# Where the first memory-key product stands: in the head loop, or among the latent products

## What is computed

```
kv  = (rmsnorm(ckv, kv_norm) @ w_ukv)           # latent products: k_nope, v of latent attention
k_c = gelu(flat @ w1) @ w2                      # compression: first product, gelu, second product
p_c = softmax(q . k_c ...)                      # compressed branch, before the head loop
s, p = scores and softmax of 3 x 6 heads        # the head loop, 18 turns
kvm = rmsnorm(mem, g_mem) @ wkv                 # memory keys and values, needed first by cross-attention
```

## Time and profile before

| | |
|---|---|
| median of 3 runs | 1771.8 us (1768.76 to 1776.57) |
| the profiled execution's own time | 1768.37 us |
| its span | 1766.5 us |
| PE busy | 1674.3 us (95%) |
| DVE busy | 1361.8 us (77%) |
| ACT busy | 1081.1 us (61%) |
| POOL busy | 210.6 us (12%) |
| mean granted clock of TensorE | 0.976 |

### The profile page before, as it was taken

How to read it: one execution, slowest core, us unless ns; L and a number is a source line. 1 busy time by engine, 2 the same in 40 slices (tenths; PEclk the granted TensorE clock), 3 DMA queues, 4 the chain that set the end, 5 groups by cost and what they waited for, 6 DMA issues and landing times.

```text
span 1766.5 us, 24349 instructions
## 1 busy us (share of the span) xinstructions
PE 1674.3 (95%) x8492; PEld 1399.3 (79%) x8492; DVE 1361.8 (77%) x1529; ACT 1081.1 (61%) x1188; POOL 210.6 (12%) x234
## 2 busy tenths in 40 slices
PE   5899999999988999969999999999999999999995
PEld 5868888888786888858888888888888888888784
DVE  5866656545577756559898898988989999989895
ACT  4345444434353454437777777777777777777773
POOL 1834001000066410030000000000000000000200
PEclk8989999999988999989999999999999999999998
DMA  9401443955431124339999999999999999999992
GB/s 356 169 24 58 151 150 140 373 190 190 176 134 48 49 97 166 119 111 423 380 374 385 373 381 369 375 385 373 374 387 371 393 378 361 389 372 356 416 375 84
DMA packets 68697, 475.94 MB, mean 269 GB/s; under 512 B 7543, under 2 KB 9079, under 8 KB 13976
## 3 DMA queue, kind: packets, MB, share of 16 engines
q1 hardware_dynamic: 63816, 453.01, 67.3%
q0 software_dynamic: 4816, 22.08, 3.1%
HBM read 461.82 MB, written 13.24 MB: 269 GB/s over the span
## 4 chain that ended last, share of the span: by engine, by line
PE 81%; DVE 7%; ACT 4%; POOL 3%; issue 2%; DMA 2%; DVEq 0%; POOLq 0%; ACTq 0%; SPq 0%
PE bank L431 24%; PE bank L433 23%; PE bank L432 23%; POOL big L2254 1%; ACT upper L474 1%; PE bank L623 1%; DVE lower L455 1%; DMA skewed_bias<-big 1%; ACT upper L451 1%; PE bank L1395 1%; DVE xel L964 1%; PE bank L1493 1%; POOL small L2254 1%; PE bank L1285 1%; PE bank L1394 1%
## 5 line engine op out<-in xcount | busy, mean ns | idle before, releaser
L480 DVE TENSOR_TENSOR lower<-ring,upper 128x2048 fp32r<-128x2048 f32 x369 | 845.4, 2292 | 144.7 <-ACT upper L474 131.5
L474 ACT ACTIVATE upper<-ring 128x2048 fp32r<-128x2048 f32 x369 | 706.4, 1915 | 108.8 <-PE bank L433 102.6
L431 PE MATMUL bank<-upper,xeu 128*128 128x512 f32 x896 | 359.7, 401 | 6.6 <-DVE xel L964 3.4
L433 PE MATMUL bank<-upper,xel 128*128 128x512 f32 x896 | 350.5, 391 | 0.0
L432 PE MATMUL bank<-lower,xeu 128*128 128x512 f32 x896 | 349.5, 390 | 0.0
L431 PE MATMUL bank<-upper,htu 128*128 128x512 f32 x536 | 209.7, 391 | 4.9 <-DVE htl L978 3.4
L433 PE MATMUL bank<-upper,htl 128*128 128x512 f32 x536 | 208.6, 389 | 0.0
L432 PE MATMUL bank<-lower,htu 128*128 128x512 f32 x536 | 208.6, 389 | 0.0
L431 PEld LDWEIGHTS bank<-upper,xeu 128*128 128x128 f32 x896 | 168.3, 188 | 38.8 <-DVE lower L480 4.1
L433 PEld LDWEIGHTS bank<-upper,xel 128*128 128x128 f32 x896 | 168.2, 188 | 35.9
L432 PEld LDWEIGHTS bank<-lower,xeu 128*128 128x128 f32 x896 | 168.7, 188 | 31.8
(11 more groups left out here) (381 smaller groups left out, 2553.6 us busy)
## 6 DMA issues: line engine op xcount, KB each, us to landing
ring<-in_weights SPq DMA_DIRECT2D x423, 1024.0 KB, 5.9
routed_rows<-g POOLq DMA_DIRECT2D x1, 4096.0 KB, 36.7
lp<-in_lparams POOLq DMA_DIRECT2D x1, 3634.5 KB, 14.4
lp<-in_lparams SPq DMA_DIRECT2D x1, 3584.0 KB, 29.5
memraw<-routed_rows POOLq DMA_DIRECT2D x7, 512.0 KB, 8.2
expert_rows<-xk POOLq DMA_DIRECT2D x7, 512.0 KB, 8.4
skewed_bias<-big SPq DMA_DIRECT2D x1, 1152.0 KB, 19.4
row<-in_mem SPq DMA_DIRECT2D x1, 1024.0 KB, 5.1
```

Source lines behind the costliest of these rows:

```text
L431: pe.matmul(to, x_up, w_up, start=start, stop=False, skip_group_check=True)
L433: return pe.matmul(to, x_lo, w_up, start=False, stop=stop, skip_group_check=True)
L474: act.activation(upper[:, third(q), :], ring[:, q % RING, :], ACT.Copy).then_inc(done, 1)
L480: dve.tensor_tensor(lower[:, q % RING, :], ring[:, q % RING, :], f32(upper[:, third(q), :]), ALU.subtract).then_inc(done, 1)
```

## The change

The job `mk0` moves in the list from turn 2 of the head loop to the place between `vm1` and `kcv`. PE: the wait for the memory's split columns and the product of chunk 7 now stand after `vm1`, ahead of the wait for `hid_ready`. ACT: the upper part of chunk 7 after the copy of `kwT`, the copy of `mk0` after `hidr`. DVE: the lower part of chunk 7 after the second rotation, ahead of `states(1)`. The splits of chunks 8 to 11 stay in turns 2, 6, 10 and 14.

```diff
@@ JOBS
-               ("vm1", "act"), ("kcv", "dve"), ("bu2", "dve"), ...
+               ("vm1", "act"), ("mk0", "act"), ("kcv", "dve"), ("bu2", "dve"), ...
-    _job(_n, _e)
+    _job(_n, _e, 7 if _n == "mk0" else None)
...
-MEMK = {2: 0, 6: 1, 10: 2, 14: 3}
+MEMK = {6: 1, 10: 2, 14: 3}
+MEM_SPLIT = {2: 1, 6: 2, 10: 3, 14: 4}
@@ PE
                     finish(f"vm{t}", ins)
+                pe.wait_ge(mem_split[l], KD)
+                features_out("mk0", MEM_FIRST, colr, memr)
                 pe.wait_ge(hid_ready[l], 1)
...
                 for i in range(LEAD):
                     scores(i)
-                pe.wait_ge(mem_split[l], KD)
@@ ACT
+                def memory_keys(m):
+                    wait_tile(act, l, f"mk{m}")
+                    drained(A(xk[:, 2 * m:2 * m + 2, :], bank(f"mk{m}")[:, :], ACT.Copy))
...
                 drained(A(kwnT[:, :], bank("kwT")[:, 0:256], ACT.Copy))
+                layer_chunk_upper(act, l, MEM_FIRST)
...
                   ACT.Copy).then_inc(hid_ready[l], 1)
+                memory_keys(0)
...
-                layer_chunk_upper(act, l, MEM_FIRST)
                 for i in range(LEAD):
                     exponentials(i)
                 for i in range(HEADS):
+                    if i in MEM_SPLIT:
+                        exponentials(i + LEAD)
+                        layer_chunk_upper(act, l, MEM_FIRST + MEM_SPLIT[i])
+                    if i == HEADS - LEAD - 1:
+                        act.wait_ge(ys_pre[l], 2)
+                        A(uT[:, :, :], uT[:, :, :], ACT.Gelu_apprx_tanh).then_inc(ys_ready[l], 1)
                     if i in MEMK:
-                        m = MEMK[i]
-                        exponentials(i + LEAD)
-                        layer_chunk_upper(act, l, MEM_FIRST + m + 1)
-                        if m == XH - 1:
-                            act.wait_ge(ys_pre[l], 2)
-                            A(uT[:, :, :], uT[:, :, :], ACT.Gelu_apprx_tanh).then_inc(ys_ready[l], 1)
-                        wait_tile(act, l, f"mk{m}")
-                        drained(A(xk[:, 2 * m:2 * m + 2, :], bank(f"mk{m}")[:, :], ACT.Copy))
+                        memory_keys(MEMK[i])
@@ DVE
                     drained(rotate(...))
+                layer_chunk_lower(dve, l, MEM_FIRST)
                 states(1)
...
-                layer_chunk_lower(dve, l, MEM_FIRST)
                 for i in range(HEADS):
...
-                    if i in MEMK:
-                        layer_chunk_lower(dve, l, MEM_FIRST + MEMK[i] + 1)
+                    if i in MEM_SPLIT:
+                        layer_chunk_lower(dve, l, MEM_FIRST + MEM_SPLIT[i])
```

More of the change, by code:

```diff
@@ L100 @@
                ("qn1", "act"), ("qr1", "dve"), ("bu1", "dve"), ("kn0", "act"), ("kn1", "act"), ("kn2", "act"), ("vm0", "act"),
-               ("vm1", "act"), ("kcv", "dve"), ("bu2", "dve"), ("qT0", "act"), ("qT1", "act"), ("qT2", "act"), ("sc", "dve"),
+               ("vm1", "act"), ("mk0", "act"), ("kcv", "dve"), ("bu2", "dve"), ("qT0", "act"), ("qT1", "act"), ("qT2", "act"), ("sc", "dve"),
                ("pcT", "act"), ("oc0", "dve"), ("oc1", "dve")):
-    _job(_n, _e)
+    _job(_n, _e, 7 if _n == "mk0" else None)
 HEADS = 18
@@ L1695, in _ @@
                     drained(A(pt[:, i % 2, 0:384], bank(f"pT{i}")[:, 0:384], ACT.Copy))
-                    if i + LEAD < HEADS and i not in MEMK:
+                    if i + LEAD < HEADS and i not in MEM_SPLIT:
                         exponentials(i + LEAD)
```

## The result

The changed kernel took **1782.4 us** (median of 8 runs, 1781.0 to 1785.7) where the kernel before took 1771.9 us in 8 runs beside it (1768.7 to 1776.6). The ratio is 1.006, with an interval of 1.0047 to 1.0072: +10.6 us, slower by 0.6%. The forecast was 1774.8 us, that is +3.0, with a range of 1766 to 1782; the measured time lies 0.4 us above the range.

What follows compares the result with a forecast made beforehand. The prediction took PE, 81% of the chain that ended last, to bound the kernel. Latent part +10.25, clock -3.85 and loop -3.4 gave +3.0 us, 1774.8 us against 1771.8, with a range of 1766 to 1782.

Steps and rivals of the forecast that it cites:

- Part 1: Latent part, up to kcv: the moved product and vm1's new wait make kcv later by 4.85 and 5.4 us.
- Part 2: From kcv to the first scores: full clock behind the dense product saves 1.95 and 1.9 us.
- Part 3: Head loop: it gives back less than the 5.76 us product taken out, 1.8 and 1.6 us.
- The first bullet: Turn 3, outputs(2): 2.9 of 5.76 us are kept, 2.8 become a new wait behind ACT's copy of pT2.
- the second: Loop after outputs(2): DVE sets the pace, gaining only its small waits for PE; outputs(12) comes 1.8 us earlier.
- the very circle: Turns 2, 6, 10 and 14: DVE's lower part waits for ACT's upper part, that for exponentials of DVE's scores.
- its ±1.3 each: First scores to pT0: the second fall of the clock is unchanged but may shift, ±1.3 us per layer.
- Rival C: Head loop: DVE and ACT bind it throughout and nothing is given back; +6.4, 1778.2 us, chance 0.1.
- rival B: After vm1: the clock falls in front of the product and the later clock saving is lost; +9.9, 1781.7 us, chance 0.12.
- B's other 1.95 us: Behind the product, kcv to first scores: the clock saving of 1.95 us per layer stays lost.
- Rival A: Head loop: PE alone bounds it, all 5.76 us return in both layers; -5.1, 1766.7 us, chance 0.13.

Runs made afterwards that it cites:

- e2: The changed kernel with mk0, in its new place, cut to 6 of its 48 matmuls: 1777.4 us, ratio 1.0043 to the kernel before.
- e1: The kernel before with mk0, in turn 2 of the head loop, cut to 6 of its 48 matmuls: 1772.3 us, ratio 1.0014.
- e4: The kernel before with DVE's group_outputs(0) of turn 6 ahead of chunk 9's lower part instead of behind it: 1770.8 us, ratio 1.0006.
- e3: The changed kernel with DVE's group_outputs(0) of turn 6 ahead of chunk 9's lower part instead of behind it: 1774.5 us, ratio 1.0031.
- e5: e3 with 20 matmuls that nobody reads ahead of the transposes of turn 3: 1775.3 us, ratio 1.0040.
- e6: e3 with chunk 7's lower part on DVE behind the two multiplications of states(1) that free vm1's bank: 1774.5 us, ratio 1.0037.
- e10: The changed kernel with the compression's gelu, table load and hidr moved on ACT behind the copy of qn0: 1780.8 us, ratio 1.0056.
- e7: e6 with mk0 cut in two, 24 matmuls ahead of kcv and 24 back in turn 2: 1768.7 us, ratio 0.9995.
- e8: The kernel before with 20 unread matmuls in the 2.46 us hole ahead of kcv: 1768.0 us, ratio 0.9988.
- e9: The kernel before with the compression's gelu, table load and hidr moved on ACT behind the copy of qn0: 1764.6 us, ratio 0.9968.

## Why the prediction was wrong

- **Part 1, the latent part: right.** Layer 1 came to +5.42 us where the working said +5.4. Layer 0 came to +5.65 where it said +4.85; the 0.8 more is DVE, which came to chunk 7's lower part 1.24 us later than the row I started from. vm1's new wait was 2.17 us in both layers, where the text of the working says "about 1.5"; its sum didn't use that wait but vm1's start, which in layer 1 came 3.08 us behind vm0's for 3.12 worked out. The product was 48 times 0.12, at full clock. e2 shows the price of vm1's wait without the product.
- **Part 2, the clock: right.** -1.86 and -1.91 for -1.95 and -1.9. e2 bears out that it hangs on the product: with six matmuls in its place the half clock is back. The forecast took the fall without the product as certain, which it isn't: in the traces with the hole and neither the whole product nor filler in it (before, e1, e2, e4), `kcv` to the first scores took 11.84 us in one layer of e1 and 12.00 in one of e4, and 13.9 to 15.3 in the other six. With the whole product ahead it took 12.0 to 12.4 us in all ten layers traced (the changed kernel, e3, e5, e6, e10). The Trainium skill's rule (TensorE: Matmul & The Clock Gate, Part 1), that the gate follows how busy the array has lately been, agrees with both rows.
- **Part 3, the loop: wrong, and in sign.** The first bullet held: 2.71 us of new wait at `outputs(2)` for 2.8, and 2.9 us of lead kept, for 2.9. The failing step is the second: "From there DVE sets the pace. It gains only its own small waits for PE", from which I went to chunk 10's upper part and on to `outputs(12)`. That walk followed DVE's masked scores and ACT's exponentials and passed over turn 6, where DVE holds something that PE needs besides scores: `group_outputs(0)`, which frees the bank of the outputs. It stood at the end of the very circle that I had described, with 0.15 us to spare, and it didn't move (29.51 to 29.63 us after `pT0`). So PE's lead of 1.75 to 1.9 us ended there, where the forecast kept it to the loop's end. e3 shows this by removing the wait: the loop came back from 64.93 to 62.73 and 63.21 us.
- **The same part, its second omission:** I gave the new waits no price in clock. I had priced the clock where a hole was closed (Part 2) and not where two were opened, 2.71 and 1.86 us long. In the loop of before PE had no wait up to `outputs(12)` and the clock was 1.00 throughout; with the two waits it fell for some 3.4 us in each layer, which is +1.6 in the trace. That the waits bring the fall is shown by the traces taken together. Twelve loops were traced with a wait of 1.8 us or more in turn 3 or at `outputs(6)` (the changed kernel, e1, e2, e3, e6, e10), and in eleven of them the clock fell at one of the waits; the twelfth is layer 0 of e6. In the twelve loops without such a wait (before, e4, e5, e7, e8, e9) no fall began. The medians haven't confirmed the price of 1.6 us (e5).
- **The sum.** The loop was off by 3.4 us per layer, 6.7 in both; 3.0 + 6.7 = +9.7 us, against +10.6 measured. The rest is within what the working allowed: the first scores to `pT0` gave +0.9 over both layers, inside its ±1.3 each. Rival C, nothing given back in the loop, was right as far as it went and stopped at +6.4: it let the loop be no worse than neutral. That is where the range ended too near. No case in my list had the loop grow when work is taken out of it, and the +9.9 of rival B is close to the result by luck: in the changed kernel's trace the clock did not fall in front of the product. B's fall does exist. It came in layer 1 of e3 and layer 0 of e10, two of the eight layers traced with the changed kernel's latent part (the changed kernel, e3, e5, e10), and cost 1.5 us each time, as B says; but the clock behind the product stayed up, so B's other 1.95 us didn't follow. How often it comes in the executions of the medians is open, and so is its share of the +10.6.
- **Rival A is refuted** by e1 (10 us of PE's work removed, 1.0014), though PE is 95% busy and 81% of the chain.

## What to carry to other kernels

When work is moved out of a loop that looks bound by the busiest engine, walk every resource that the other engines hand back in each turn, buffers read and freed as well as data produced, and note its slack: the one with the least slack takes the lead away, here one with 0.15 us. Then price every new stillness in clock as well as in time. And before filling a hole on the critical engine with work from elsewhere, ask what makes the hole: here the wait was a table load and a gelu which could run 8 us sooner in an idle gap of ACT, and that gave 6 us where filling the hole cost 10.

## What the runs showed of the hardware that was not expected

- **The clock falls in different places in executions of the same work.** In e4 the hole ahead of `kcv` is 2.46 us in both layers; in layer 0 the clock stayed at 1.00 behind it (`kcv` to the first scores 12.00 us), in layer 1 it was 0.60 from 561 to 568.5 us (15.34 us). In e1 the loop's half clock came in turns 3 to 5 in one layer and in turn 7 in the other. A price for a fall read from one stretch is good to about ±1.5 us.
- **A trace without a fall isn't a faster kernel.** e5 had the clock at 1.00 in both loops and its median is no better than e3's, whose trace shows two falls.
- **DVE beside POOL: the one that starts second waits for the other.** The lower part of a chunk took 2.29 us in turn 6 of the kernel before and 2.86 us in turn 6 of the changed one, in both layers, and POOL worked beside it in either. What differs is who came first. In the changed kernel POOL's second multiplication began at 614.18 us, 0.01 ahead of DVE, and took its usual 0.72; DVE took 0.57 longer. In the kernel before DVE began at 604.45, 0.02 ahead of POOL, and took its usual 2.29; POOL's multiplication took 2.86 instead of some 0.73, and ended 0.6 us behind DVE. That is the row `603.77 3.55` above, for both multiplications, against 1.41 in the changed kernel. The 0.57 us took the 0.45 that DVE had gained up to there. The Trainium skill (SBUF — State Buffer, SBUF: two separate sides) calls the shared port an exclusive lock that the first to start holds for its whole instruction; both traces agree with it, with these numbers.
